# Two 64-row experts moved from the first expert stage beside the first looped job and the last job

## The reference, cut to what matters

```python
def swiglu(x, w_gu, w_down, width):
    h = x @ w_gu
    return (jax.nn.silu(h[..., :width]) * h[..., width:]) @ w_down

for e in range(N_EXPERTS):      # 8 experts, d = 1024, width 3584
    out = out + gate[..., e:e + 1] * swiglu(x, w_gu[e], w_down[e], D_EXPERT)
```

## Time and profile before

| | |
|---|---|
| time, median of 3 runs | 1698.66 us (1695.87 to 1700.48) |
| span of the profiled execution, first to last instruction | 1691.0 us |
| what lies outside the span, by that median | 7.7 us |
| PE busy | 1599.3 us, 95% |
| DVE busy | 1024.0 us, 61% |
| ACT busy | 753.5 us, 45% |
| moved by DMA | 466.84 MB |

### The profile page before, as it was taken

One profiled execution on the slowest core, in us unless ns is written; L12 is line 12 of the kernel. 1 busy time (PEld: TensorE's weight loads), 2 busy tenths in 40 slices (PEclk: granted clock), 3 DMA queues, 4 the chain that ended last, 5 costly groups with the idle time before them and its releaser, 6 DMA issues.

```text
span 1691.0 us, 27595 instructions
## 1 busy us (share of the span) xinstructions
PE 1599.3 (95%) x10689; PEld 1213.1 (72%) x10689; DVE 1024.0 (61%) x1314; ACT 753.5 (45%) x834; POOL 142.9 (8%) x247
## 2 busy tenths in 40 slices
PE   8999999999999999999899979786999999999997
PEld 6768999999966667763445535554788888888785
DVE  4678766657665555651313212331888888888897
ACT  4226433435452223341213211231777777777675
POOL 1241000000113540020000000000000000000300
PEclk9999999999999999989999999898999999999998
DMA  9959655444232530089999999999999999999992
GB/s 234 265 153 314 168 149 162 149 121 153 78 97 64 168 115 2 1 318 398 403 398 405 408 402 400 404 403 398 411 389 358 402 382 352 405 371 364 391 392 99
DMA packets 232253, 466.84 MB, mean 276 GB/s; under 512 B 25205, under 2 KB 121620, under 8 KB 232129
## 3 DMA queue, kind: packets, MB, share of 16 engines
q1 hardware_dynamic: 217246, 426.81, 69.4%
q0 software_dynamic: 11744, 31.62, 5.9%
q10 hardware_dynamic: 3155, 6.93, 1.1%
HBM read 445.78 MB, written 19.99 MB: 275 GB/s over the span
## 4 chain that ended last, share of the span: by engine, by line
PE 81%; DMA 9%; DVE 6%; ACT 3%; issue 1%; SPq 0%; POOL 0%; ACTq 0%; DVEq 0%; POOLq 0%
PE ps L2896 10%; PE ps L3052 9%; PE ps L3053 9%; PE ps L3054 9%; PE ps L2298 7%; PE ps L2300 7%; PE ps L2299 7%; DMA raw<-in_moe_w_gu 5%; PE ps L2889 3%; DMA raw<-in_moe_w_down 3%; PE ps L2890 2%; PE ps L2891 2%; PE ps L2712 2%; PE ps L2675 2%; PE ps L2751 2%; PE ps L2411 1%
## 5 line engine op out<-in xcount | busy, mean ns | idle before, releaser
L2149 DVE TENSOR_TENSOR w_lo<-raw,w_hi 128x2048 fp32r<-128x2048 f32 x168 | 383.9, 2292 | 67.0 <-ACT w_hi L1356 66.1
L1356 ACT ACTIVATE w_hi<-raw 128x2048 fp32r<-128x2048 f32 x168 | 322.6, 1921 | 133.7 <-PE ps L3054 117.1
L2155 DVE TENSOR_TENSOR w_lo<-raw,w_hi 128x2048 fp32r<-128x2048 f32 x42 | 96.3, 2292 | 226.6 <-ACT w_hi L1363 226.2
L2298 PE MATMUL ps<-x_hi,w_hi 128*128 128x306 f32 (+1 forms) x656 | 201.9, 308 | 1.2 <-DVE x_lo L1625 0.6
L2300 PE MATMUL ps<-x_lo,w_hi 128*128 128x306 f32 (+1 forms) x656 | 199.1, 304 | 0.0
L2299 PE MATMUL ps<-x_hi,w_lo 128*128 128x306 f32 (+1 forms) x656 | 198.8, 303 | 0.0
L3052 PE MATMUL ps<-w_hi,g_hi 128*128 128x512 f32 x448 | 176.8, 395 | 6.2 <-DVE w_lo L2149 6.2
L3053 PE MATMUL ps<-w_lo,g_hi 128*128 128x512 f32 x448 | 175.2, 391 | 0.0
L3054 PE MATMUL ps<-w_hi,g_lo 128*128 128x512 f32 x448 | 175.2, 391 | 0.0
L2896 PE MATMUL ps<-raw,g_s 128*32 128x128 f32 (+3 forms) x1920 | 164.7, 387 | 9.3 <-DMA raw<-in_moe_w_gu 9.2
L1491 DVE TENSOR_TENSOR w_lo<-raw,w_hi 128x2048 fp32r<-128x2048 f32 (+4 forms) x129 | 135.4, 1097 | 54.4 <-ACT w_hi L1069 54.0
(11 more groups left out here) (503 smaller groups left out, 2533.6 us busy)
## 6 DMA issues: line engine op xcount, KB each, us to landing
raw<-in_moe_w_gu SPq DMA_DIRECT2D x224, 1024.0 KB, 9.9
raw<-in_moe_w_down SPq DMA_DIRECT2D x112, 1024.0 KB, 9.9
raw<-in_ffn_w_gu SPq DMA_DIRECT2D x44, 512.0 KB, 5.2
raw<-in_conv_w_in SPq DMA_DIRECT2D x16, 512.0 KB, 9.3
raw<-in_ffn_w_down SPq DMA_DIRECT2D x16, 512.0 KB, 4.1
kvn<-in_cache_ckv POOLq DMA_DIRECT2D x64, 128.0 KB, 3.5
kvn<-in_cache_ckv SPq DMA_DIRECT2D x64, 128.0 KB, 2.9
rows_in<-zrow POOLq DMA_DIRECT2D x13, 512.0 KB, 10.5
```

The lines of the kernel that those rows point to most:

```text
L1356: nc.scalar.activation(w_hi[:, u % SPLIT], raw[:, u % RAW], ACT.Copy).then_inc(hi_done, 1)
L2149: V.tensor_tensor(w_lo[:, u % SPLIT], raw[:, u % RAW], w_hi[:, u % SPLIT].bitcast(F32), ALU.subtract).then_inc(lo_done, 1)
L2155: V.tensor_tensor(w_lo[:, n % F_SPLIT], first_raw(k), w_hi[:, n % F_SPLIT].bitcast(F32), ALU.subtract).then_inc(lo_done, 1)
L2298: nc.tensor.matmul(out, hi, xh, start=start, stop=False, skip_group_check=True)
```

## The change

H and C (the 32-row expert) alone stay in the first stage, 84 units. Job 0 runs alone as before. Job 1 runs as a *pair* with A, and the last job as a pair with B; jobs between them run alone. A pair has 84 units: the 42 wide ones of the job in `ORDER`, and 42 narrow ones of A or B, now in seven steps of 512 hidden columns, put into the gaps between the wide ones by `pair_schedule`. `BESIDE[k]` holds what stands ahead of wide unit k. The 6 places of `raw` are shared by both kinds; `AT[k]` is the position of wide unit k among the 84.

```diff
+def pair_schedule():
+    gaps = []
+    for s in range(NARROW_STEPS):
+        stages = [[("gate", s, 0)], [("gate", s, 1)], [("up", s, 0)], [("up", s, 1)], [("turn", s, 0)]]
+        if s == 0:
+            gaps += [stages[0] + stages[1]] + stages[2:]
+        else:
+            gaps += [[("down", s - 1, 0), ("down", s - 1, 1)] + stages[0]] + stages[1:]
+    gaps.append([("down", NARROW_STEPS - 1, 0), ("down", NARROW_STEPS - 1, 1)])
+    return [[], []] + gaps + [[]] * (JOB_UNITS + 1 - 2 - len(gaps))
...
+        def fetch_pair(j, at, x, next_rows):
...
+            for p, (kind, s, part, k) in enumerate(PAIR_SEQ):
+                if p < RAW or PAIR_SEQ[p - RAW][3] is not None:
+                    done = p - RAW if p < RAW else PAIR_SEQ[p - RAW][3]
+                    sp.wait_ge(lo_done, j * JOB_UNITS + (SPLIT_FIRST + U_MOE + done + 1))
+                else:
+                    sp.wait_ge(unit_used, job_base(j, extra) + (p - RAW + 1))
```

The pair on ACT:

```diff
+        def pair(j, x, last):
+            base = job_base(j, last)
+            for k in range(JOB_UNITS + 1):
+                if k + AHEAD < JOB_UNITS:
+                    split_in_pair(k + AHEAD, j, last)
...
+                for kind, s, part, p in BESIDE_AT[k]:
+                    n = narrow(x, s)
+                    if kind == "gate" and part == 1:
+                        act.wait_ge(unit_used, base + p + 1)
+                        nc.scalar.activation(sg_p[:, 0:n], gate_bank(x, n), ACT.Silu).then_inc(f_sp, 1)
+                    if kind == "turn":
+                        act.wait_ge(f_t, TURNS_BEFORE[x] + s + 1)
+                        nc.scalar.activation(hT_s[:, 0:n // P], ...).then_inc(f_ts, 1)
```

The pair on DVE:

```diff
+        def pair(j, x, last):
+            for k in range(JOB_UNITS + 1):
+                if k + AHEAD < JOB_UNITS:
+                    split_moe(k + AHEAD, j, AT[k + AHEAD])
...
+                for kind, s, part, p in BESIDE_AT[k]:
+                    if kind == "up" and part == 1:
+                        n = narrow(x, s)
+                        v.wait_ge(unit_used, base + p + 1)
+                        v.wait_ge(f_sp, SILUS[x] + s + 1)
+                        V.tensor_tensor(hh_p[:, 0:n], sg_p[:, 0:n], up_bank(x, n), ALU.mult).then_inc(f_hp, 1)
```

The pair on PE; `turn_narrow` waits for `f_hp` and makes two transposes of `hh_p`:

```diff
+        def beside(j, x, kind, s, part, p, last):
+            if kind == "turn":
+                turn_narrow(x, s)
+                return
+            if kind == "up" and part == 0:
+                pe.wait_ge(f_sp, SILUS[x] + s + 1)
+            if kind == "down" and part == 0:
+                pe.wait_ge(f_ts, SILUS[x] + s + 1)
+            place_at = (U_MOE + p) % RAW
+            pe.wait_ge(raw_ready[place_at], job_raw_target(p, j, last))
+            small_unit(raw[:, place_at], kind, x, s, part).then_inc(unit_used, 1)
...
-        with pe.Fori(0, last_job) as j:
-            job(j)
-        job(last_job, True)
+        job(0, 2)
+        pair(1, "A", False)
+        with pe.Fori(2, last_job) as j:
+            job(j, 3)
+        pair(last_job, "B", True)
```

More of the change, by code:

```diff
@@ L111 @@
 HALF = SLOTS // 2
-SMALL_AFTER = (2, 2, 1, 2, 2, 1, 2)
 FIRST_JOBS = 4
 SMALL = "ABC"
+NARROW_STEPS = 2 * STEPS - 1
 def wide(x, s):
-    return 1 if x == "H" else HALVES[s]
+    return HALVES[s] if x == "C" else 1
 def first_jobs_schedule():
[L123 to L127, removed]
-    seq = []
[L129 to L141, removed]
-        else:
[L143 to L150, removed]
@@ new lines, in first_jobs_schedule @@
+    large, small = [], []
+    for s in range(NARROW_STEPS):
+        for i, unit in enumerate([("gate", "H", s, 0), ("gate", "H", s, 1), ("up", "H", s, 0), ("up", "H", s, 1)]):
+            large.append(([("turn", "H", s - 1, 0)] if i == 0 and s else []) + [unit])
+        if s:
+            large += [[("down", "H", s - 1, part)] for part in range(2)]
+    for s in range(STEPS):
+        parts = range(2 * HALVES[s])
+        small += [[("gate", "C", s, part)] for part in parts] + [[("up", "C", s, part)] for part in parts] + [[("turn", "C", s, 0)]]
+        downs = [("down", "C", s, part) for part in parts]
+        small += [downs[i:i + 2] for i in range(0, len(downs), 2)]
@@ new lines, in first_jobs_schedule @@
+    seq = []
+    for i, stage in enumerate(large):
+        seq += stage
+        if 1 <= i < len(large) - 2:
+            for _ in range(2 if i == 3 else 1):
+                seq += small.pop(0)
+    assert len(small) == 1
+    seq += [("turn", "H", NARROW_STEPS - 1, 0)] + small[0] + [("rows", "H", 0, 0)]
+    return seq + [("down", "H", NARROW_STEPS - 1, part) for part in range(2)]
+def pair_schedule():
+    gaps = []
+    for s in range(NARROW_STEPS):
+        stages = [[("gate", s, 0)], [("gate", s, 1)], [("up", s, 0)], [("up", s, 1)], [("turn", s, 0)]]
+        if s == 0:
+            gaps += [stages[0] + stages[1]] + stages[2:]
+        else:
+            gaps += [[("down", s - 1, 0), ("down", s - 1, 1)] + stages[0]] + stages[1:]
+    gaps.append([("down", NARROW_STEPS - 1, 0), ("down", NARROW_STEPS - 1, 1)])
+    return [[], []] + gaps + [[]] * (JOB_UNITS + 1 - 2 - len(gaps))
@@ L165 @@
     if kind_ == "turn":
+        assert at_unit - 1 not in TURNS
         TURNS[at_unit - 1] = (x_, s_)
@@ L1384, in _ @@
             if e == ROWS_AFTER:
[L1385 to L1389, removed]
+                rows_upper(1, 0, 7)
             if e in GATES:
@@ L1445, in _ @@
-        with act.Fori(0, last_job) as j:
-            job(j)
+                    nc.scalar.activation(comb[:], ps[:, 3, 0:3 * P], ACT.Copy)
+                    nc.scalar.activation(comb_b, ps[:, 1, 0:3 * P], ACT.Copy).then_inc(last_act, 1)
+                for kind, s, part, p in BESIDE_AT[k]:
[5 more added lines that the diff above has]
+                        act.wait_ge(f_t, TURNS_BEFORE[x] + s + 1)
+                        nc.scalar.activation(hT_s[:, 0:n // P], gate_bank(x, n).rearrange("p (c s) -> p c s", s=SLOTS), ACT.Copy).then_inc(f_ts, 1)
+                    if kind == "down" and part == 1 and s == NARROW_STEPS - 1:
+                        act.wait_ge(unit_used, base + p + 1)
+                        nc.scalar.activation(y_b[:] if last else y_s[x], ps[:, 7, 0:D // TILES[x]], ACT.Copy).then_inc(f_fl, 1)
@@ L1448, in _ @@
+        job(0)
+        pair(1, "A", False)
+        with act.Fori(2, last_job) as j:
+            job(j, True)
         act.dma_start(gbc[:], ln_g[1, 1:2].broadcast_to([P, D])).then_inc(fin_ld, 16)
         act.dma_start(bbc[:], ln_b[1, 1:2].broadcast_to([P, D])).then_inc(fin_ld, 16)
-        job(last_job, True)
+        pair(last_job, "B", True)
         act.wait_ge(last_pe, 2)
@@ L2978, in large_unit, with small_unit @@
             return m
-        def small_unit(k, kind, x, s, part):
-            w, n = first_raw(k), wide(x, s)
+        def small_unit(w, kind, x, s, part):
+            n = wide(x, s)
             if kind == "down":
@@ new lines, in job_unit @@
+        def job_unit(j, k, last=False):
+            kind, s, part = ORDER[k]
+            u = U_MOE + k
+            n = HALVES[s]
+            if k == 0:
+                pe.wait_ge(m_gl, j + 1)
+            if kind == "gate" and part == 0 and s >= 1:
+                pe.wait_ge(m_sg, j * STEPS + s)
+            if kind == "up" and part == 0 and s >= 1:
+                pe.wait_ge(m_h, j * STEPS + s)
+            if kind == "down" and part == 0:
+                pe.wait_ge(m_hTl, j * STEPS + (s + 1))
+                if s == 0:
+                    pe.wait_ge(m_yc, j + 1)
+            pe.wait_ge(lo_done, j * JOB_UNITS + (SPLIT_FIRST + u + 1))
+            for i in range(4):
+                if kind == "down":
+                    bank, c = 4 + i % 2, 2 * part + i // 2
+                    hi, lo = hT_hi[:, (8 if s == STEPS - 1 else 0) + c], hT_lo[:, (8 if s == STEPS - 1 else 0) + c]
+                    start, stop = s == 0 and c == 0, s == STEPS - 1 and c == 4 * n - 1
+                else:
+                    bank, c = (0 if kind == "gate" else 2) + i % n, (4 // n) * part + i // n
+                    hi, lo = g_hi[:, c], g_lo[:, c]
+                    start, stop = c == 0, c == DC - 1
+                wh, wl = w_hi[:, job_slot(k), 512 * i:512 * i + 512], w_lo[:, job_slot(k), 512 * i:512 * i + 512]
+                m = split_product(ps[:, bank, :], hi, lo, wh, wl, start, stop)
+                if last and k == JOB_UNITS - 1 and i == 2:
+                    m.then_inc(last_pe, 1)
+            m.then_inc(unit_used, 1)
@@ new lines, in pair @@
+        def pair(j, x, last):
+            for k in range(JOB_UNITS + 1):
+                for kind, s, part, p in BESIDE_AT[k]:
+                    beside(j, x, kind, s, part, p, last)
+                if k == JOB_UNITS:
+                    break
+                if ORDER[k][0] == "up" and ORDER[k][2] == 0 and ORDER[k][1] >= 1:
+                    pe.wait_ge(m_hTl, j * STEPS + ORDER[k][1])
+                job_unit(j, k, last)
+                if k in TURN_AFTER:
```

(1 more changed line is left out.)

366 lines of the change are left out of this document (225 added, 141 removed).

## The result

The changed kernel takes 1902.22 us (median of 4 runs, 1897.00 to 1903.29) against 1698.17 us: a ratio of 1.1195, 95% interval 1.1169 to 1.1221. It is 204 us slower; I had forecast 163 more, 1862 us. The span of the profiled execution is 1895.3 us where I had 1854.

What follows compares the result with a forecast made beforehand. Before, DMA bounds the first stage and PE the jobs; in pairs, waits hold both. 256 + 119.8 + 305 + 119.8 + 305 + 9 = 1114.6 us against 951.5, 163 more: 1862 us, range 1785 to 1925.

Steps and rivals of the forecast that it cites:

- What bounds, and the work of a pair: In a pair: without waits DMA would bound, with 84 transfers in 219 us against 207 us of PE work.
- The two waits: Each narrow step: PE waits 7.6 us for hh_p at the turn and 4.4 us for the silu ahead of u0.
- The silu's wait: Ahead of u0: g1's silu stands on ACT behind position 20's split; PE idles 4.4 us, 3 in a pair's start.
- 2.6 for each one behind it: Fetches queued in a pair: each lands 2.6 us after the one ahead, so 17 to 20 land at 23.4 to 31.2.
- a fetch alone: A single weight fetch: 5.7 us to land, in jobs 4.9 to 9.0; taken as 5.5 with 0.2 to issue.
- The clock: PE after idling in a pair: turn and W 10 take 5.3 us, not 3.3; 0.6 us added for the second wait.
- the gathering: In the last job it cost 8 us before; 6 us were left for it, part falling into waits.
- The first stage: H's wide units with C units beside them: 256 us, bounds 245 and 275.
- the products at the end: 6 more products ahead of those at L3087: 3 us more.
- Only the turn waits: Rival for the pairs: silu in time and clock holds, a pair takes 263 us, total 1778 us; chance 0.09.
- The clock stays low: Rival for the pairs: PE at 1.2 GHz from turn to silu, a pair takes 362 us, total 1976 us; chance 0.03.
- Balance works: Rival for the pairs: PE's waits are covered and DMA sets the pace, 937 us of experts, total 1684 us; chance 0.05.

Runs made afterwards that it cites:

- Experiment one: Changed kernel with ACT and DVE taking the narrow expert's small instructions ahead of the split of wide unit k + 2: 1769.65 us, ratio 1.0418.
- four: Changed kernel with only the gaps changed, the first gate unit moved from behind the two downs to ahead of the second gate unit: 1880.72 us, ratio 1.1072.
- experiment nine: experiment six with the wide job's own turn copies (hT_hi on ACT, hT_lo on DVE) also ahead of the split: 1701.78 us, ratio 1.0028.
- Experiment eight: Changed kernel plus 24 zero products ahead of a turn and 20 ahead of u0 in later steps of each pair: 1877.95 us, ratio 1.1065.
- experiment six: Experiment one with ACT's copy of the narrow turn (hT_s) one index earlier: 1709.75 us, ratio 1.0074.

## Why the prediction held, and where it was off

**What bounds, and the work of a pair: right.** 84 transfers at 2.61 us are 219 us, and with the waits gone the pair with A took 223.8 at a DMA share of 1.02. I had put PE's work in a pair at 207 us; with the clock at 1.00 throughout it was 206.72.

**The two waits: right in place, count and cause.** The turn waited 7.5 us on average (105.2 in 14) where I had 7.6. That close a match is partly luck: it was 6.6 in the pair with A and 8.4 in that with B. Experiment one took `hh_p` and `sg_p` from behind the splits and both waits nearly went; four moved the late unit by one position and the turn's wait shrank.

**The silu's wait: mis-sized.** I had 4.4 us, and 3 in a first step; 79.3 us in 14 are 5.7. The term that was too small is "2.6 for each one behind it". In the step shown, after the idle time, SP issued four fetches from 1186.69 on, each when its place was free and those ahead of it in the queue had left, and they landed so (DMA issues by stretch: one issued before 1187.5, one before 1189.5, two before 1194; the last column is us from issue to landing):

```profile
raw<-in_moe_w_gu SPq DMA_DIRECT2D x1, 1024.0 KB, 5.3
...
raw<-in_moe_w_gu SPq DMA_DIRECT2D x1, 1024.0 KB, 7.9
...
raw<-in_moe_w_gu SPq DMA_DIRECT2D x2, 1024.0 KB, 9.8
```

The 9.8 is the median of two: taken one by one, the third took 8.8 us and the fourth 10.8. The first landed at 1192.0 and the split of the second began only at 1196.30, 4.3 us on where I had 2.6. The fourth was there 15.0 us after the first down unit freed a place (1186.5 to 1201.5), against 13.5 in my working (17.7 to 31.2). I had also left out that ACT takes the job's own silu, 1.00 us at L1505, ahead of `sg_p` in some steps. The 5.7 us that I called a fetch alone weren't quite that, since DMA was moving 422 GB/s in the microsecond in which it was issued. And the fit that I weighed against it, in the section "Anatomy of one DMA" of the page "DMA: Bandwidth & Descriptors" in the Trainium skill, is stated there for transfers that GpSimd issues; these are issued by SP, so it did not bear on them.

**The clock: mis-sized.** I allowed 2.0 us at a turn, and 0.6 at a silu, since after 3 us of idling PE had come back at either level. The measured cost is PE's busy time in the changed kernel less that in experiment nine: 233.54 - 206.72 = 26.8 us in the pair with A and 234.97 - 211.55 = 23.4 in that with B, 50 us where I had 35. The second figure is a lower bound, since in experiment nine itself the granted clock of that pair was 0.97. All 14 waits for a silu were of 4.5 to 7.0 us, and the up unit behind each took 3.0 to 3.7 us, 11 of them 3.6 to 3.7, which is the 1.2 GHz level. The section "HAM oscillation" of the page "TensorE: Matmul & The Clock Gate" in the Trainium skill, by which the second wait too brings the array down every time, would have added some 19 us; the traces agree with it, with 15 more than I allowed. Experiment eight shows the same from the other side, with 22 to 24 us back where 8 of 14 steps were filled.

**The sum, term by term.** Pair with A: 206.7 work, 46.4 at the turns (I had 53), 40.0 for the silus (29), 26.8 for the clock (18), together 320 for my 305. (My terms add up to 307; the path that I followed held 2 us less of PE's work than the 207.) So the turns came 7 us better than forecast and the silus and the clock 20 worse, and the total was nearer than they were. Pair with B: 211.6, 58.8, 39.3 and 23.4 are 333 for my 311 (the terms: 313). Its turn waits are longer in the first two steps, 10.66 and 12.20 us. At the first of them some DVE instructions of the gathering (1578.55 to 1580.42 us) stand between `w_lo` and `hh_p`; around the second the row transfers on POOL's queue share the DMA engines, and a fetch of weights took a median of 13.3 us. I had 6 us for the gathering; the pair with B took 13 more than that with A, and still 9 more in experiment nine. No run took the gathering away, so what share of the 9 each of its parts has is open. The first stage (254.2 for 256) and the products at the end (2.9 for 3) were right. The first fetch left 3.0 us later than before; it stood at 723.4 to 727.3 us in the ten kernels with this first stage, and I have no cause for that.

**The rivals.** *Only the turn waits*, 1778 us, fell: there was a wait for the silu in all 14 steps. *The clock stays low*, 1976 us, fell: the granted clock was back at 1.00 between 1185 and 1190 us, in the step shown. *Balance works*, 1684 us, fell for the change as made, and not even the kernel that realises the balance got there. From the first fetch to the last wide product, experiment nine has 953.1 us, and 3 more at the end, where that rival has 937: 3.9 in the first stage, 2.8 in the lone jobs, 4.8 in the pair with A, 13.9 in that with B, less the 6 that it had apart for gathering. Those 953.1 us stand against 951.5 before (from the first fetch to the first closing product in both), and with the 3 at the end that is the 0.3%: the 20 us that balance can give are paid out again in those places. In none of the orders tried did the pairing make the kernel faster.

## What to carry to other kernels

Before work is put beside other work, write down for each in-order queue what stands ahead of every small instruction that another engine waits for: here 0.4 us instructions behind a split that waited for its transfer cost 192 of the 204 us, and moving them, with no work taken away, gave these back (experiment six). If that transfer's place comes free only by work behind the same wait, the idle times of PE and DMA add up instead of covering each other. What more than 6 places would do with the order as first made, no run shows. Fix all such places together, since one engine's order alone gave 17 and 53 us of 133, the wait only moving on.

## What the runs showed of the hardware beyond what I had expected

- Four fetches of 1 MB, issued within 5 us into idle queues (in the step shown), took 5.3, 7.9, 8.8 and 10.8 us to land, so that the fourth was there 15.0 us after the first place came free.
- PE was at the lower level behind each of the 14 silu waits, of 4.5 us and more, with 3.0 to 3.7 us for 16 products that take 1.95 at full clock; 20 zero products in such a wait kept it at the upper level in all eight cases.
- The fall can come late. After 4.80 us of idling the last turn of the pair with A still took 0.44 us, as at full clock (1394.47 us), and the third matmul behind it was at the lower level (0.63 us, from 1395.37).
- At a turn, 24 zero products with 2.5 to 4.3 us of idling behind them didn't always hold the clock: it was granted at 0.58 to 0.60 behind three of eight.
